# Gathering 42 tokens' expert rows instead of 32, three picks at a time, in a two-block transformer kernel

## The reference, cut to what matters

```python
v1, i1 = lax.top_k(s1, 16); v2, i2 = lax.top_k(s2, 16)        # per token and head, over 128 keys each
vs, ci = lax.top_k(v1[..., :, None] + v2[..., None, :], 16)   # of the 256 sums
eidx  = e1 * 128 + e2                                         # which expert
gates = softmax(vs)
act = gelu(einsum('tkd,td->tk', expert_u[eidx], xn))          # xn = rms_norm(h) * gain
h   = h + einsum('tk,tkd->td', act * gates, expert_v[eidx])
```

## Time and profile before

| | |
|---|---|
| median of 3 runs | 2959.25 us (2958.08 to 2959.38) |
| the profiled execution's own time | 2959.44 us |
| its span, first to last instruction | 2957.7 us |
| mean granted TensorE clock | 0.998 of full speed |
| busy share PE / PEld / DVE / ACT / POOL | 98% / 89% / 67% / 47% / 20% |
| DMA | 692.88 MB, 234 GB/s mean |

### The profile page before, as it was taken

How to read it: one execution, slowest core, us unless ns; L and a number is a source line. 1 busy time by engine, 2 the same in 40 slices (tenths; PEclk the granted TensorE clock), 3 DMA queues, 4 the chain that set the end, 5 groups by cost and what they waited for, 6 DMA issues and landing times.

```text
span 2957.7 us, 41749 instructions
## 1 busy us (share of the span) xinstructions
PE 2910.0 (98%) x16599; PEld 2625.5 (89%) x16599; DVE 1969.9 (67%) x2753; ACT 1388.9 (47%) x1992; POOL 593.0 (20%) x555
## 2 busy tenths in 40 slices
PE   8999999999999999999999999999999999999999
PEld 7998778888888887978789999999999999999999
DVE  5556654444444445464568999677787888888876
ACT  4355544444444444354444444444455555555553
POOL 2000000000000000150004888488710000000000
PEclk9999999999999999999999999999999999999999
DMA  8554356666665554544567888899997888888764
GB/s 292 162 168 151 115 175 222 224 234 231 226 197 183 187 198 140 176 153 156 177 218 252 226 224 224 279 328 336 343 375 266 314 324 323 324 316 316 260 215 141
DMA packets 244456, 692.88 MB, mean 234 GB/s; under 512 B 46569, under 2 KB 98825, under 8 KB 210880
## 3 DMA queue, kind: packets, MB, share of 16 engines
q1 hardware_dynamic: 194560, 600.81, 59.4%
q0 software_dynamic: 47168, 86.54, 10.5%
q10 hardware_dynamic: 2560, 3.21, 0.4%
HBM read 654.70 MB, written 33.69 MB: 233 GB/s over the span
## 4 chain that ended last, share of the span: by engine, by line
PE 49%; DVE 2%; ACT 0%; issue 0%; ACTq 0%; DVEq 0%
PE banks L2231 16%; PE banks L2286 15%; PE banks L2232 8%; PE banks L2287 7%; PE banks L2307 1%; PE banks L2309 1%; PE banks L2308 1%; DVE weights_lo L195 1%; PE banks L2250 0%; DVE peer_features L376 0%; DVE top_index L2049 0%; ACT weights_hi L188 0%; PE banks L2259 0%; PE banks L2275 0%; DVE row_gates L2063 0%
## 5 line engine op out<-in xcount | busy, mean ns | idle before, releaser
L195 DVE TENSOR_TENSOR weights_lo<-weights,weights_hi 128x1024 fp32r<-128x1024 f32 (+4 forms) x1080 | 1228.4, 1179 | 702.8 <-ACT weights_hi L188 700.7
L188 ACT ACTIVATE weights_hi<-weights 128x1024 fp32r<-128x1024 f32 (+4 forms) x1080 | 1046.5, 1017 | 1370.6 <-PE banks L417 639.7
L2231 PE MATMUL banks<-peer_features,weights_hi 128*128 128x448 f32 (+1 forms) x2304 | 734.8, 378 | 6.1 <-DVE weights_lo L195 6.1
L415 PE MATMUL banks<-weights_hi,features_hi 128*128 128x512 f32 (+3 forms) x1600 | 608.0, 380 | 26.2 <-DVE weights_lo L195 23.0
L2232 PE MATMUL banks<-peer_features,weights_lo 128*128 128x224 f32 (+1 forms) x2304 | 610.2, 265 | 0.0
L417 PE MATMUL banks<-weights_hi,features_lo 128*128 128x512 f32 (+3 forms) x1600 | 602.5, 377 | 0.0
L416 PE MATMUL banks<-weights_lo,features_hi 128*128 128x512 f32 (+3 forms) x1600 | 602.4, 377 | 0.0
L2286 PE MATMUL banks<-peer_features,weights_hi 128*128 128x448 f32 x1568 | 492.5, 374 | 0.0
L2231 PEld LDWEIGHTS banks<-peer_features,weights_hi 128*128 128x128 f32 x2304 | 432.0, 187 | 48.6 <-DVE weights_lo L195 8.7
L2232 PEld LDWEIGHTS banks<-peer_features,weights_lo 128*128 128x128 f32 x2304 | 439.2, 191 | 0.0
L2197 POOL DMA_INDIRECT expert_gates<-peer_choice x224 | 399.4, 1783 | 182.3 <-DVEq L2071 102.8
(11 more groups left out here) (400 smaller groups left out, 2729.3 us busy)
## 6 DMA issues: line engine op xcount, KB each, us to landing
weights<-in_expert_u SPq DMA_DIRECT2D x128, 1024.0 KB, 6.3
weights<-in_expert_v SPq DMA_DIRECT2D x128, 1024.0 KB, 6.4
weights<-in_w_ffn_gate SPq DMA_DIRECT2D x44, 1024.0 KB, 5.2
weights<-in_w_ffn_up SPq DMA_DIRECT2D x44, 1024.0 KB, 5.2
weights<-in_w_ffn_down SPq DMA_DIRECT2D x44, 1024.0 KB, 4.8
weights<-in_w_in SPq DMA_DIRECT2D x48, 900.0 KB, 5.0
weights<-in_w_out SPq DMA_DIRECT2D x32, 1024.0 KB, 5.1
weights<-in_w_in SPq DMA_DIRECT2D x24, 704.0 KB, 4.2
```

Of the source, the lines that this page charges most:

```text
L188: act.activation(hi[:, k, n], raw[:, k, n], ACT.Copy).then_inc(self.hi_ready, 1 + skip)
L195: last = dve.tensor_tensor(lo[:, k, n], raw[:, k, n], hi[:, k, n].bitcast(F32), ALU.subtract)
L415: pe.matmul(out, xh, wh, start=first, stop=False)
L2231: pe.matmul(self.bank(n % 3, 2 * cols), wh[:, k, :], F[:, k, :, 0:cols], start=(k == 0), stop=False)
```

## The change

42 tokens become row tokens and 214 remain dense. With 42 tokens only three picks fit in 128 partitions (`GROUPS` = 3, `USED` = 126), and 128 picks take 43 gathers (`RUNS`) of 126 rows for each table in place of 32 of 128 rows. Each gathered row is now summed, and later added, in one DVE operation of 2048 numbers instead of two of 1024. The `SUM` steps begin two steps earlier and their last twelve lie in v's units; `ADD` begins ten steps later. Since 42 is not a multiple of 32, lists of picks and gates are rearranged on DVE and moved across partitions by six small DMAs from ACT's queue at step 70, and three more at step 9 move the tokens' scale. The first three gathers now stand after all early scatters (116 of them). The row tokens' own gates are scattered to cells behind the dense table, by two more small tables made on POOL at the start of the layer.

```diff
-    WQ, ROWS, ZEROED = 384, 32, 8
+    WQ, ROWS, ZEROED = 384, 42, 8
...
-        SUM = [*range(78, 142)]
-        DOTS = SUM[-1] + 1
-        free = [s for s in range(V0 + 17, V0 + 118) if (s - V0) % 16 not in (0, 5, 6, 8, 10, 14)]
-        ADD = [free[k * len(free) // (2 * ROWS)] for k in range(2 * ROWS)]
+        GROUPS = P // ROWS
+        RUNS, USED = -(-SLOTS // GROUPS), GROUPS * ROWS
+        MINE = slice(P - ROWS, P)
+        SUM = [76 + c * 21 // 10 for c in range(31)] + [V0 - 1 + 2 * c for c in range(12)]
+        DOTS = SUM[-1] + 2
+        free = [s for s in range(V0 + 27, V0 + 118) if (s - V0) % 16 not in (0, 5, 6, 8, 10, 14)]
+        ADD = [free[k * len(free) // RUNS] for k in range(RUNS)]
...
                     if t == ROW_TILE:
-                        for quarter in range(4):
-                            row_gate_part = row_gate[quarter * ROWS:quarter * ROWS + ROWS, 0, part * 8:part * 8 + 8]
-                            k = part * HP * TOPK + quarter * 8
-                            last = dve.tensor_copy(row_gate_part, gates_of[P - ROWS:P, t, k:k + 8])
-                        ch(last)
+                        ch(dve.tensor_copy(lists[2][:, part * HP * TOPK:(part + 1) * HP * TOPK],
+                                           gates_of[:, t, part * HP * TOPK:(part + 1) * HP * TOPK]))
+                        if part == PARTS - 1:
+                            turned = lambda x: x.rearrange("p (q c) -> p c q", q=GROUPS)
+                            full = SLOTS // GROUPS * GROUPS
+                            for of, to in ((picked, picked_turned), (lists[2], lists[3])):
+                                dve.tensor_copy(turned(to)[:, 0:SLOTS // GROUPS, :],
+                                                of[:, 0:full].rearrange("p (c q) -> p c q", q=GROUPS))
+                                last = dve.tensor_copy(turned(to)[:, SLOTS // GROUPS, 0:SLOTS - full], of[:, full:SLOTS])
+                            ch(last)
+                            dve.sem_inc(listed, 1)
...
                     def gather(c):
-                        if c % 8 == 0 and c < ROWS:
-                            pool.wait_ge(listed, c // 8 + 1)
+                        if c == 0:
+                            pool.wait_ge(moved, 16 * 2 * GROUPS)
...
-                    early, mixed = 124, 4
-                    for n, cell in enumerate(cells[:early]):
+                    early, mixed = 116, 4
+                    for cell in cells[:early]:
                         scatter(*cell)
-                        if n < BUFS:
-                            gather(n)
-                    for c in range(BUFS, 2 * ROWS):
+                    for c in range(BUFS):
+                        gather(c)
+                    for c in range(BUFS, 2 * RUNS):
                         gather(c)
...
+                        if s == RET + 60:
+                            act.wait_ge(listed, 1)
+                            for q in range(GROUPS):
+                                mine, to = slice(q * RUNS, (q + 1) * RUNS), slice(q * ROWS, (q + 1) * ROWS)
+                                act.dma_start(pick[to, :], picked_turned[MINE, mine]).then_inc(moved, 16)
+                                act.dma_start(row_gate[to, 0, :], lists[3][MINE, mine]).then_inc(moved, 16)
...
-                        for k in [k for k, at_step in enumerate(SUM) if at_step == s]:
-                            c, part = divmod(k, 2)
-                            if part == 0:
-                                dve.wait_ge(gathered[c % BUFS], 16 * (c // BUFS + 1))
-                            row, x_row = [y[:, part * D // 2:(part + 1) * D // 2] for y in (rows[:, c % BUFS, :], xg)]
-                            dve.tensor_tensor_reduce(row, row, x_row, 1.0, 0.0, ALU.mult, ALU.add, dots[:, part, c:c + 1])\
-                                .then_inc(row_summed, 1)
...
+                        for c in [c for c, at_step in enumerate(SUM) if at_step == s]:
+                            dve.wait_ge(gathered[c % BUFS], 16 * (c // BUFS + 1))
+                            row = rows[0:USED, c % BUFS, :]
+                            dve.tensor_tensor_reduce(row, row, xg[0:USED, :], 1.0, 0.0, ALU.mult, ALU.add, dots[:, 0, c:c + 1])\
+                                .then_inc(row_summed, 2)
+                        for c in [c for c, at_step in enumerate(ADD) if at_step == s]:
+                            dve.wait_ge(gathered[(RUNS + c) % BUFS], 16 * ((RUNS + c) // BUFS + 1))
+                            row, weight, to = rows[0:USED, (RUNS + c) % BUFS, :], row_gate[:, 0, c:c + 1], row_sum[0:USED, :]
+                            dve.wait_ge(row_summed, 2 * (RUNS + c))
```

More of the change, by code:

```diff
@@ L2001, in peer @@
             att = self.att[:, :, :, :].rearrange("p a t h -> p (a t h)")
-            pick = att[:, 0:ROWS].bitcast(U32)
+            pick = att[:, 0:RUNS].bitcast(U32)
+            lists = [rows[:, 1, 256 * n:256 * n + GROUPS * RUNS] for n in range(4)]
+            picked, picked_turned = lists[0].bitcast(U32), lists[1].bitcast(U32)
             sems = lambda *names: [self.sem("peer_" + n) for n in names]
@@ L2175, in _ @@
                     self.pool_chain.on(pool)(pool.iota(token_i[:, :], pattern=[[P, NT]], base=0, channel_multiplier=1))
-                    self.pool_chain.on(pool)(pool.tensor_copy(token[:, :], token_i[:, :]))
+                    ch = self.pool_chain.on(pool)
+                    pool.memset(by_key[:, 0, :], float(DENSE))
+                    pool.memset(by_key[:, 1, :], float(NKEYS * DENSE))
+                    pool.memset(past[:, 0:1], float(P * NKEYS * DENSE - (NT - 1) * P))
+                    pool.memset(past[:, 1:2], float(P))
+                    ch(pool.tensor_copy(token[:, :], token_i[:, :]))
+                    for n in range(2):
+                        step = by_key[:, n, ROW_TILE:ROW_TILE + 1]
+                        pool.affine_select(out=step, in_=step, pattern=[[0, 1]], compare_op=ALU.is_ge, fill=0.0,
+                                           base=P - ROWS - 1, channel_multiplier=-1)
+                    ch(pool.affine_select(out=past[:, :], in_=past[:, :], pattern=[[0, 2]], compare_op=ALU.is_ge, fill=0.0,
+                                          base=ROWS - P, channel_multiplier=1))
+                    ch(pool.tensor_tensor(out=token[:, ROW_TILE:ROW_TILE + 1], in0=token[:, ROW_TILE:ROW_TILE + 1], in1=past[:, 0:1],
+                                          op=ALU.add))
                     pool.sem_inc(counted, 1)
@@ L2186, in gather @@
                             pool.wait_ge(xg_made, 1)
-                        pool.indirect_dma_start(out=rows[:, c % BUFS, :], out_offset=None, in_=rows_d if c < ROWS else values_d,
-                                                in_offset=bass.IndirectOffsetOnAxis(ap=pick[:, c % ROWS:c % ROWS + 1], axis=0))\
+                        pool.indirect_dma_start(out=rows[0:USED, c % BUFS, :], out_offset=None, in_=rows_d if c < RUNS else values_d,
+                                                in_offset=bass.IndirectOffsetOnAxis(ap=pick[0:USED, c % RUNS:c % RUNS + 1], axis=0))\
                             .then_inc(gathered[c % BUFS], 16)
@@ L2391, in _ @@
                             if j == 0:
[L2392 removed]
+                                act.wait_ge(row_tokens, 16 * (GROUPS + 1))
                                 act.wait_ge(self.squares.sem, self.squares.at(2))
@@ L2507, in _ @@
                         if s == 10:
-                            dve.wait_ge(row_tokens, 80)
-                            ch(dve.tensor_tensor(xg[:, :], xg[:, :], rows[:, 0, :], ALU.mult))
+                            dve.wait_ge(row_tokens, 16 * (GROUPS + 1))
+                            ch(dve.tensor_tensor(xg[0:USED, :], xg[0:USED, :], rows[0:USED, 0, :], ALU.mult))
+                            for to in (lists[1], lists[3]):
+                                ch(dve.memset(to[:, GROUPS * RUNS - 1:GROUPS * RUNS], 0.0))
@@ L2518, in _ @@
-                        for k in [k for k, at_step in enumerate(ADD) if at_step == s]:
-                            c, part = divmod(k, 2)
-                            if part == 0:
-                                dve.wait_ge(gathered[(ROWS + c) % BUFS], 16 * ((ROWS + c) // BUFS + 1))
-                            row, to = [y[:, part * D // 2:(part + 1) * D // 2] for y in (rows[:, (ROWS + c) % BUFS, :], row_sum)]
-                            weight = row_gate[:, 0, c:c + 1]
-                            if c > 0 or part > 0:
-                                dve.wait_ge(row_summed, 2 * ROWS + max(k - 1, 0))
+                        for c in [c for c, at_step in enumerate(SUM) if at_step == s]:
[3 more added lines that the diff above has]
+                                .then_inc(row_summed, 2)
@@ L2528, in _ @@
                             else:
-                                last = dve.scalar_tensor_tensor(out=to, in0=row, scalar=weight, in1=to, op0=ALU.mult, op1=ALU.add)
```

(4 more changed lines are left out.)

51 lines of the change are left out of this document (27 added, 24 removed).

## The result

The changed kernel takes 3110.57 us (median of 4 runs, 3100.72 to 3118.0), the kernel before 2959.22 us beside it: ratio 1.051, 95% interval 1.048 to 1.0541. It is 151 us slower. The forecast was 2930 us, 29 us faster, with a range up to 2947. It was wrong in size and sign.

The account below looks back on a forecast made before the run. PE sets the pace, with DVE at 88% in v's units. Narrower matmuls -34.1, DVE's row work +3.0, score loads +1 and picks +1 sum to -29.1 us: 2930 us from 2959.4, range 2912 to 2947.

Parts of the forecast that it names:

- rival C: Gathered rows land too late, so DVE stops at most of the 43 ADDs: 2973 us at 1 us each; chance 0.05.
- the stride: v's wide matmul reads at stride 1712 bytes in place of 1792: bounded at 0 to 7 us, taken as 0.
- B: DVE or transfers eat much of the gain through overloads, late score loads and v's matmuls: 2940 to 2950 us; chance 0.18.
- Narrower matmuls: PE's pairs in both tables: 20 columns off the wide matmul save 34.1 us, the narrow one gives 0; other bound 51.2.
- on its floor: Below some 230 columns a matmul's time, 107 to 108 ns, stops following its columns, so narrowing the narrow one gives nothing.
- A: Columns count in full in PE's matmuls: -51.2 us, units of 4.82 us, 2917 us in all; chance 0.17.
- DVE's row work: Whole sums and ADDs on DVE, 95% busy in v's ADD steps, make PE wait: +3.0 us, bounds 2 and 10.
- The walk: Step-by-step check of DVE's work, steps 100 to 265: PE waits at ten steps of v, 3.0 us in all.
- The picks: Tail steps of the row tile, with changed small copies and slightly longer stalls: +1 us, bounds -1 and +4.
- The scores' loads: DVE's scaling waits longer for score loads, issued two shorter units ahead under higher traffic: +1 us, bounds 0 and 8.
- Queues: POOL's gathers and scatters, SP's wait for the last scatter, ACT's small DMAs: costed at nothing, 0 to 5 us.

Follow-up runs that it names:

- the two padding rows: The changed kernel with its gathers widened from 126 to 128 partitions, the two added rows never read: 2961.27 us, ratio 1.001 to the kernel before.
- the best kernel: The changed kernel with 128-partition gathers, twelve scatters moved up, every second score load one fill earlier and ADDs kept off busy steps: 2933.54 us, ratio 0.9915.
- the first two edits: On the changed kernel with 128-partition gathers, twelve scatters moved into POOL's idle time and every second score load issued one fill earlier: 2940.48 us, ratio 0.9934.
- the third edit: On top of the first two edits, the 43 ADD steps moved to steps not full of other work: 2933.54 us, ratio 0.9915.
- the edit to the scatters: On the changed kernel with 128-partition gathers, twelve scatters moved into POOL's idle time after the first three gathers: 2949.13 us, ratio 0.9971.

## Why the prediction was wrong

**The step that failed** is the landing time of a gather, on which rival C and the terms for the score loads and the queues rest. I took the landing of a 126-row gather from the 128-row ones (9.3 us, 13.3 at most), since two rows less could only shorten it, and set the point from which C decides at 22 us (0.8 us late at each `ADD`; by its own sum, 29.1 us over 43, it is 0.7). No row of the trace before has another width, so that was a price without a row, and it needed a bound as the stride got one. Measured were 14.1 us in the median and 40.9 at most. At 128 partitions, with the same 86 gathers, they are 9.9 and 16.2: then the 0.05 for C would have been fair. And the sum had no term at all for what slow gathers do to the transfers beside them: the median fill of table v went from 6.4 to 12.4 us, the score loads from 9.6 to 16.4 (7.6 and 11.4 with 128 partitions). That this one step is behind 149 of the 151 us is shown by the two padding rows; how these divide over rows, fills and scores is not.

**C's mechanism** was half of it. Rows did come late, at 15 of the sums for u (73.1 us), but at no `ADD`: it named the wrong table. Weight fills and score loads came late as well, which no rival held. B named the score loads, but priced them at 8 us.

**Narrower matmuls.** Forecast 305 ns a pair and -34.1 us; measured 307 ns, 4.91 us a unit against 5.01, which is -26 us for 256 units. But in v 39 of the best kernel's 127 units take only 4.85 to 4.87 us, and by the mean of all units without stalls it is -15 us in u and -17 in v. The mechanism was right: the narrow matmul is on its floor, and A, at 0.17, is out. The size was 2 to 8 us off. The N/2.4 + 2.5 ns of the Trainium skill ("TensorE: Matmul & The Clock Gate", Back-to-back issue gap) is given there for matmuls in isolation. For a stream of matmuls with a weight load each, as here, the section itself says that it counts too little when N is small, so the 313 ns are no evidence against the page.

**DVE's row work.** Forecast 2.26 us an `ADD` and 2.27 a sum, measured 2.35 and 2.29; DVE's share in v forecast 95%, measured 94% (422.81 of 450). The walk named ten places where PE would wait, 3.0 us in all. In the kernel with the first two edits PE waits at five of them (6, 22, 62, 78 and 110 of v), 2.6 us in all, and the third edit, which empties three of the five, gave 3.3 us in v's units. This holds only where transfers are on time; in the changed kernel it is buried.

**The picks.** Forecast +1 us, measured +0.6: PE's waits in u's units up to step 76 come to 9.2 us before and 9.8 in the best kernel.

**The scores' loads.** +1 with 8 as the bound. With 128 partitions 8.7 us by the time and 10.6 by v's units, with 126 a wait of 77.5 us on DVE. I had the two units that shrink and the higher traffic in the text, and still took the low end. The one wait of 2.06 us said that the slack was used up already.

**Queues.** Nothing, with 5 us as the bound; 10.5 us in the two units that the edit to the scatters repairs. I had the last scatter at 2145 us. It was 2164: the sets take 11.0 us, not 10.5, which over 27 of them is 13 us, and the first begins at 1870 in place of 1865. SP's wait was 16.8 us.

**The sum,** for the kernel with 128 partitions: -26 for the units, 10.5 and 9 for the stalls, some 6 before and in the query projection, which gives -0.5 of the -2.5 us in its span. With the terms for loads, queues and DVE repaired it is 25 us faster, near the 29 forecast; that is no success of the forecast, since three edits that are no part of the change had to give back the loads' and the queues' terms, which it held at 1 us and which measured some 21. The 149 us on top are the width of the gathers.

## What to carry to other kernels

Before you let a DMA run on a number of partitions that is not the one measured, time that number: here 126 in place of 128 cost 2.5% to 5% and 119 cost 8%, while two padding rows to reach 128 took the loss away. A DMA share that rises while GB/s falls is the sign to look for. When a transfer that shares its engines with critical ones changes, price the critical ones too; and where a load is already waited for once, take any further delay in full.

## What the runs showed of the chip that was not expected

- A row's 8 KB packet of the software queue takes 309 ns in the median in gathers on 128 partitions, and 461 to 560 ns on 96, 112, 119, 120 and 126. In the changed kernel it is 480 ns. Why even 96 and 112 partitions lose 0.5% and 0.6% was not found; which engine gets which row can't be read from the records, only how many packets run at once.
- Odd gathers slow the packets of other queues: the fills' 8 KB packets, 356 ns on average from 1880 to 2190 us in the kernel before, take 383 beside gathers of 96 or 112 partitions, 443 beside 126, 455 beside 120 and 492 beside 119.
- A matmul pair of 448 and 160 columns takes 320 ns in most units, one of 448 and 224 takes 313 and one of 428 and 214 takes 307. A shorter matmul under a 128-column weight load made the pair longer. Not explained.
- After PE had been idle for 9 us it ran at 1.2 GHz for some 4 us (the changed kernel's timeline at 2402.89 us), which costs about 2 us on top of the wait. The mean granted clock was 0.976 against 0.998.
- The start of the first query unit lay at 1464 to 1466.5 us in some kernels and at 1469.5 to 1472 in others (the changed one, its 128-partition form, that with the first two of the three edits, and the best one with 126-partition gathers), though the edits between them touch nothing before it. Most of the 3 to 8 us between them are in the untouched feed-forward stage (516 or 517 matmuls in 1017 to 1137 us in place of 525 to 529), and no run here tells why. Differences between kernels of less than that are read from the units, not from the time.
